# Stick-breaking attention with its row tiles taken from the last to the first

## Chip, core and metric

One core of one Trainium2 chip. The metric is the device time of one execution in microseconds (us), the median of several runs.

## What is computed

One decoder layer over 1024 prompt rows and 8 sample rows. What matters here:

```
q, k, v, u = rmsnorm(x) @ w_in            # q, k normalised per head; 8 heads of 64
z[i, j]    = q[i] . k[j] / 8 + bias       # strictly causal: j < i
a[i, j]    = sigmoid(z[i, j]) * product over j < l < i of sigmoid(-z[i, l])
h          = x + concat(a @ v, pool(u)) @ w_out
m          = rmsnorm(h)                   # then the router: top 1 of 4 groups, top 2 of 8 experts
h         += the two experts' outputs, weighted by their gates
y          = h + sigmoid(rmsnorm(h) @ w_ple_gate) * (p @ w_ple_proj)
```

## The kernel before

All rows lie in nine row tiles of 128: tile 0 holds the 8 samples, tiles 1 to 8 the prompt. The kernel has stages with a barrier of all engines between them: the projection (to 300 us), the attention stage (here), the experts (from 634 us) and a last stage (from 1245 us).

**The attention stage.** Its work is cut into units, in the list `units` (L804). A unit is (t, hp, g): the queries of row tile t (1 to 8), a pair of heads hp (0 to 3), and a group g of up to four key blocks (L808). Tiles 1 to 4 have one group and so four units each; their width is 128, 256, 384 and 512 columns. Tiles 5 to 8 have two groups and so eight units each: group 1 (width 128 to 512), then group 0 (width 512). That makes 48 units, numbered n = 0 to 47. Each unit goes through these steps:

- "scores" (L944, and the causal mask at L949 in the group that holds the diagonal) on TensorE; then four sigmoids on ScalarE (L1060, L1061); then two scans and a product on VectorE (L1134, L1139). It is done three units ahead: while unit n is finished, the scores of unit n + 3 are made.
- "turn": transposes of the weights into `p_at` on TensorE (L957), copied to `aT` by ScalarE (L1068).
- "values": the product with v into `p_o` (L967). After a tile's last unit ScalarE copies `p_o` to `mixT` ("attn", L1074).

**The jobs.** Beside the units stand nine jobs, one for each row tile: pieces 1 to 4 are the product with `w_out` in two halves of 512 columns (L993); VectorE adds the residual row (L1153) and multiplies by the norm's gain (L1155); "rows" transposes the result through `p_at` (L1006), ScalarE copies it to `hT` and takes the sum of squares (L1080, L1083), and GpSimd stores h and m to HBM (L912, L913) and loads the residual rows of the job after next (L915); piece 6 is the router's product (L1000, logits copied at L1172). Job number j is for row tile `jobs[j]`. Job j stands beside the units of one tile; in a tile of four units the pieces are spread as (1, 2), (3, 4), rows, 6; in one of eight units as 1, 2, 3, 4, nothing, rows, 6, nothing (`shares`, L823). The ninth job, j = 8, comes alone after the last unit (`tail`, L849). Every engine follows a plan written out by hand (L846 to L848): for a unit n in TensorE's order: turn n, scores n + 3, rows, pieces, values n.

**Queues.** SP's queue waits at L877 to L879 until job 7's h and m rows have landed in HBM, and only then loads `pT_raw` (L880, 1 MB), the first expert's gate and up weights (after all scores, L882) and down weights (after all values, L885), 2 MB each. When job 8's second half is multiplied (L888) it loads the second expert's three (L891 to L893). Then it stores the nine tiles of `p_times_w_ple_proj` (L900), whose products (L1016 to L1018) TensorE makes in `p_sc[T % 2]` after job 8; ScalarE copies each to `y_sb[T % 2]` (L1102), from T = 2 on only after the store of tile T - 2 has landed (L1100). VectorE meanwhile computes the routing tables (L1207 to L1268), and GpSimd gathers the first experts' rows (L927).

In job 8 ScalarE's plan holds the copy `pT_hi` (L1087), which waits for `pT_raw`, and VectorE's the difference `pT_lo` (L1158), in front of the residual add (L1153).

Of the kernel before, what the change touches and what calls it, by code (L numbers as in the profile page):

```python
# [17 lines left out]
T_ALL = 1 + SEQ // P  # L18
ROWS = T_ALL * P
AW = 512  # L20
H, HD = 8, 64
# [51 lines left out]
def build(nc, A, O):  # L73
# [20 lines left out]
    with ctx:  # L94
# [604 lines left out]
        GRP = 4  # L699
# [96 lines left out]
        at_done, at_copied, o_done, attn_copied = sem("aT_done"), sem("aT_copied"), sem("heads_done"), sem("attn_copied")  # L796
        w_done, w_copied = sem("p_w_filled"), sem("p_w_copied")
# [3 lines left out]
        s_c2 = sem("const2_loaded")  # L801


        units = [(t, hp, g) for t in range(1, T_ALL) for hp in range(H // 2) for g in reversed(range((t + GRP - 1) // GRP))]  # L804

        def unit(n):
            t, hp, g = units[n]
# [2 lines left out]

        def pair(n):
            t, hp, _ = units[n]
            return (t - 1) * (H // 2) + hp

        def last_of_pair(q):
            return max(n for n in range(len(units)) if pair(n) == q)
# [1 line left out]

        jobs = list(range(T_ALL))
        jobs_in = {t: [t - 1] for t in range(1, T_ALL)}
        shares = {4: [(1, 2), (3, 4), (5,), (6,)], 8: [(1,), (2,), (3,), (4,), (), (5,), (6,), ()]}  # L823

        def pieces_in(n):
# [12 lines left out]
        for n in range(len(units)):  # L838
            t, hp, g = units[n]
# [12 lines left out]
        fills, turns_to, n_turns = {}, {}, 0  # L852
        for what, arg in plan:
            if what == "piece":
                j, k = arg
# [13 lines left out]
        with nc.Block() as block:  # L869
# [62 lines left out]
            def _(pe):  # L932
                for what, arg in plan:
                    if what == "scores":
                        t, hp, g, blocks, w = unit(arg)
                        if arg >= 2:
                            pe.wait_ge(sig_done, arg - 1)
                        masked = blocks[-1] == t - 1
                        sc = p_sc[arg % 2]
                        half = w // 2 if w > 2 * P else w  # L940
                        for c in range(0, w, half):
                            for hh in range(2):
                                rows = slice(HD * hh, HD * hh + HD)
                                ins = pe.matmul(sc[:, hh * CHUNK + c:hh * CHUNK + c + half], qT[rows, hp, (t - 1) * P:t * P],  # L944
                                                kT[rows, hp, g * CHUNK + c:g * CHUNK + c + half], start=True,
                                                stop=not masked or c + half < w)
                        if masked:
                            for hh in range(2):
                                ins = pe.matmul(sc[:, hh * CHUNK + w - P:hh * CHUNK + w], ident_b[:], mask_b[:], start=False, stop=True)  # L949
                        ins.then_inc(sc_done, 1)  # L950
                    elif what == "turn":
                        t, hp, g, blocks, w = unit(arg)
                        pe.wait_ge(a_done, arg + 1)
                        pe.wait_ge(at_copied, turns_to["turn", arg])
                        for hh in range(2):
                            for i in range(len(blocks)):
                                ins = pe.transpose(p_at[:, hh * CHUNK + i * P:hh * CHUNK + (i + 1) * P], beta[arg % 3][:, hh, i * P:(i + 1) * P], ident[:])  # L957
                        ins.then_inc(at_done, 1)
                    elif what == "values":
                        t, hp, g, blocks, w = unit(arg)  # L960
                        if hp == 0 and t >= 2:
                            pe.wait_ge(attn_copied, t - 1)
                        pe.wait_ge(at_copied, turns_to["turn", arg] + 1)
                        for i, b in enumerate(blocks):
                            for hh in range(2):
                                h = 2 * hp + hh
                                ins = pe.matmul(p_o[HD * hh:HD * hh + HD, hp * P:(hp + 1) * P], v_sb[:, b + 1, h * HD:(h + 1) * HD],  # L967
                                                aT[arg % 2][:, hh, i, :], start=(i == 0 and blocks[-1] == t - 1),
                                                stop=(i == len(blocks) - 1 and g == 0))
                        ins.then_inc(o_done, 1)  # L970
                    elif what == "piece":
                        j, k = arg
                        T = jobs[j]

                        def begin(name):
                            if fills[j, name] > 0 and not (j == len(jobs) - 1 and name == "h1"):
                                pe.wait_ge(w_copied, fills[j, name])

                        if k in (1, 2, 3, 4):
                            n = (k - 1) // 2  # L980
                            if k == 1:
                                begin("h0")
                                pe.wait_ge(s_wout, 16 * KD)
                                if T > 0:
                                    pe.wait_ge(attn_copied, T)
                            if k == 3:
                                begin("h1")
                            for kk in range(4 * ((k - 1) % 2), 4 * ((k - 1) % 2) + 4):
                                if kk < 4:
                                    lhs = (mixT[T % 2] if T > 0 else mixT_s)[:, kk, :]  # L990
                                else:
                                    lhs = mixp[:, kk - 4, T * P:(T + 1) * P]
                                ins = pe.matmul(bank(j, f"h{n}"), lhs, w_out[:, kk, n * CHUNK:(n + 1) * CHUNK], start=(kk == 0), stop=(kk == 7))  # L993
                            if k in (2, 4):
                                ins.then_inc(w_done, 1)
                        if k == 6:
                            begin("logits")
                            pe.wait_ge(at_copied, turns_to["rows", j] + 1)
                            for kk in range(KD):
                                ins = pe.matmul(p_w[:, 0:NR], hT[:, kk, :], w_rt[:, kk, :], start=(kk == 0), stop=(kk == KD - 1))  # L1000
                            ins.then_inc(w_done, 1)
                    elif what == "rows":
                        pe.wait_ge(m_ready, 2 * arg + 2)
                        pe.wait_ge(at_copied, turns_to[what, arg])
                        for kk in range(KD):
                            ins = pe.transpose(p_at[:, kk * P:(kk + 1) * P], m_sb[arg % 2][:, kk * P:(kk + 1) * P], ident[:])  # L1006
                        ins.then_inc(at_done, 1)
# [39 lines left out]
            def _(act):  # L1047
                for what, arg in act_plan:
                    if what == "scores":
                        t, hp, g, blocks, w = unit(arg)  # L1050
# [18 lines left out]
                                       p_at[:].rearrange("p (a n) -> p a n", a=2)[:, :, 0:w], ACT.Copy).then_inc(at_copied, 1)  # L1069
                    elif what == "attn":  # L1070
                        act.wait_ge(o_done, max(n for n in range(len(units)) if units[n][0] == arg) + 1)
                        if arg >= 3:
                            act.wait_ge(w_done, fills[jobs.index(arg - 2), "h1"] + 1)
                        act.activation(mixT[arg % 2][:].rearrange("p c n -> p (c n)"), p_o[:], ACT.Copy).then_inc(attn_copied, 1)  # L1074
                    elif what == "rows":
                        j, T = arg, jobs[arg]
                        act.wait_ge(at_done, turns_to[what, arg] + 1)
                        if j >= 1:
                            act.wait_ge(w_done, fills[j - 1, "logits"] + 1)
                        act.activation(hT[:].rearrange("p c n -> p (c n)"), p_at[:], ACT.Copy).then_inc(at_copied, 1)  # L1080
                        if j >= 1:
                            act.wait_ge(h_ss, j)
                        act.activation(x_r[j % 2][:], h_sb[j % 2][:], ACT.Square, accum_out=h_sq[:, T:T + 1]).then_inc(h_ss, 1)  # L1083
                    elif what == "piece" and arg == (T_ALL - 1, 1):
                        act.wait_ge(s_pt, 16)
                        act.wait_ge(o_done, len(units))
                        act.activation(pT_hi[:], pT_raw[:], ACT.Copy).then_inc(p_hi, 1)  # L1087
                    elif what == "piece" and arg == (T_ALL - 1, 4):
                        act.wait_ge(s_wp, 16)
                        act.wait_ge(w_done, fills[T_ALL - 1, "h1"] + 1)  # L1090
                        act.activation(wp_hi[:], wp_raw[:], ACT.Copy).then_inc(p_hi, 1)

                        act.activation(h_rs[:, 1, 0:1], h_sq[:, 0:1], ACT.Sqrt)
# [984 lines left out]
```

## Time and profile before

| | us |
|---|---|
| median of 3 runs (lowest, highest) | 1370.99 (1369.13, 1376.37) |
| profiled execution, own time | 1377.2 |
| its span | 1375.4 |
| TensorE busy | 1293.3 (94%) |
| VectorE busy | 866.8 (63%) |
| ScalarE busy | 779.7 (57%) |
| GpSimd busy | 201.4 (15%) |
| mean granted TensorE clock | 0.972 of full |

The profile has a record of each instruction with its start and length, the granted clock of TensorE, and the DMAs. Full clock is 2.4 GHz; the other level it shows is half of that. A row of the timeline is: start, length, engine, line, operation, output<-inputs and shapes, the number of instructions merged, and in square brackets the idle time of the engine before it with what ended it. A 4-byte matmul shows as more than one instruction, so 16 rows of L993 are one half of a job. PEld is TensorE's weight load. SPq is SyncE's queue issuing a DMA.

### The profile page before, as it was taken

The page shows a single profiled execution, that of the slowest core. Times are in us where ns is not written, and L with a number is a line of the kernel's source. Part 1 is how long each engine was busy: PE and PEld are TensorE (multiplying, and loading weights), DVE is VectorE, ACT ScalarE, POOL GpSimd, SP SyncE. Part 2 cuts the span into 40 slices and gives each one's busy share as a digit, 9 for nine tenths or more (in the row PEclk, how much of TensorE's full clock was granted, in tenths as well). Part 3 has the DMA queues.
Part 4 walks back from the last instruction along what each step waited for, and adds up shares of the span by engine and source line. Part 5 has one row for each costly group of instructions (what it writes and reads, how often), then busy time and mean ns, then how long its engine had stood idle before and what let it go on. Part 6 is the DMA issues. An engine that isn't in the chain of part 4 may idle for free. (4 is left out here: it accounts for less than half of the span.)

```text
span 1375.4 us, 18490 instructions
## 1 busy us (share of the span) xinstructions
PE 1293.3 (94%) x6698; PEld 953.9 (69%) x6698; DVE 866.8 (63%) x787; ACT 779.7 (57%) x887; POOL 201.4 (15%) x207
## 2 busy tenths in 40 slices
PE   7999899999999999888999999999999999964998
PEld 4767576674565566556777778877777778853886
DVE  5434411123545667464888888888888888846554
ACT  5434311123445567535777777777778777834453
POOL 3001100000000000001122222222222222110000
PEclk9999899999999999999999999999999999986999
DMA  8756656461111111295799999999999999923552
GB/s 301 266 204 240 221 168 228 156 221 48 46 47 46 47 47 47 100 392 217 290 369 375 381 388 381 376 379 370 374 364 377 376 382 370 350 88 126 200 210 110
DMA packets 63866, 332.66 MB, mean 242 GB/s; under 512 B 12543, under 2 KB 12831, under 8 KB 49838
## 3 DMA queue, kind: packets, MB, share of 16 engines
q1 hardware_dynamic: 45374, 281.29, 52.7%
q0 software_dynamic: 18432, 50.56, 10.1%
q8 instruction: 38, 0.62, 0.2%
q14 instruction: 22, 0.18, 0.0%
HBM read 309.08 MB, written 39.74 MB: 254 GB/s over the span
## 5 line engine op out<-in xcount | busy, mean ns | idle before, releaser
L1336 DVE TENSOR_TENSOR w_lo<-w_gate,w_hi 128x2048 fp32r<-128x2048 f32 x64 | 146.6, 2293 | 32.8 <-ACT w_hi L1332 32.8
L1336 DVE TENSOR_TENSOR w_lo<-w_down,w_hi 128x2048 fp32r<-128x2048 f32 x64 | 146.4, 2287 | 12.4 <-ACT w_hi L1332 12.4
L1134 DVE TENSOR_TENSOR_SCAN keep<-keep 128x512 f32<-128x512 f32 (+3 forms) x96 | 88.6, 964 | 87.9 <-ACT beta L1061 87.9
L1336 DVE TENSOR_TENSOR w_lo<-w_up,w_hi 128x2048 fp32r<-128x2048 f32 x64 | 143.6, 2285 | 0.0
L407 PE MATMUL p_z<-w_in_hi,xT_hi 128*128 128x512 f32 (+1 forms) x288 | 119.7, 415 | 9.5 <-DVE w_in_lo L532 9.5
L1332 ACT ACTIVATE w_hi<-w_down 128x2048 fp32r<-128x2048 f32 x64 | 122.6, 1915 | 0.0
L1332 ACT ACTIVATE w_hi<-w_up 128x2048 fp32r<-128x2048 f32 x64 | 122.4, 1913 | 0.0
L1332 ACT ACTIVATE w_hi<-w_gate 128x2048 fp32r<-128x2048 f32 x62 | 118.5, 1913 | 0.0
L408 PE MATMUL p_z<-w_in_lo,xT_hi 128*128 128x512 f32 (+1 forms) x288 | 114.6, 398 | 0.0
L409 PE MATMUL p_z<-w_in_hi,xT_lo 128*128 128x512 f32 (+1 forms) x288 | 114.4, 397 | 0.0
L1347 PE MATMUL p_g<-w_hi,xeT_hi 128*128 128x512 f32 x256 | 104.1, 407 | 2.5 <-DVE xeT_lo L1555 2.5
L1347 PE MATMUL p_y<-w_hi,hiddenT_hi 128*128 128x512 f32 x256 | 104.1, 407 | 2.1 <-DVE hiddenT_lo L1581 2.1
L1347 PE MATMUL p_u<-w_hi,xeT_hi 128*128 128x512 f32 x256 | 102.9, 402 | 0.0
L1068 ACT ACTIVATE aT<-p_at 128x1024 f32<-128x1024 f32 (+3 forms) x48 | 39.5, 824 | 109.8 <-PE p_at L957 109.8
L1348 PE MATMUL p_g<-w_hi,xeT_lo 128*128 128x512 f32 x256 | 101.2, 395 | 0.0
L1348 PE MATMUL p_y<-w_hi,hiddenT_lo 128*128 128x512 f32 x256 | 100.9, 394 | 0.0
L1348 PE MATMUL p_u<-w_hi,xeT_lo 128*128 128x512 f32 x256 | 100.2, 392 | 0.0
L1434 POOL DMA_INDIRECT expert_rows<-y,idx_y x32 | 81.5, 2548 | 29.5 <-POOL idx_y L1431 28.2
L407 PEld LDWEIGHTS p_z<-w_in_hi,xT_hi 128*128 128x128 f32 (+1 forms) x288 | 51.8, 180 | 40.0 <-issue 27.5
L1353 PE MATMUL p_g<-w_lo,xeT_hi 128*128 128x512 f32 x256 | 70.2, 396 | 0.0
L1353 PE MATMUL p_y<-w_lo,hiddenT_hi 128*128 128x512 f32 x256 | 70.2, 397 | 0.0
L1353 PE MATMUL p_u<-w_lo,xeT_hi 128*128 128x512 f32 x256 | 68.9, 391 | 0.0
(261 smaller groups left out, 2506.1 us busy)
## 6 DMA issues: line engine op xcount, KB each, us to landing
w_gate<-in_w_experts SPq DMA_DIRECT2D x32, 2048.0 KB, 12.8
w_up<-in_w_experts SPq DMA_DIRECT2D x32, 2048.0 KB, 15.9
w_down<-in_w_experts SPq DMA_DIRECT2D x32, 2048.0 KB, 8.0
v_sb<-in_cache_kT SPq DMA_DIRECT2D x64, 256.0 KB, 6.6
w_in_raw<-in_cache_v SPq DMA_DIRECT2D x64, 256.0 KB, 3.8
xT_raw<-in_xT_all POOLq DMA_DIRECT2D x16, 512.0 KB, 5.5
y_loaded<-expert_rows SPq DMA_DIRECT2D x8, 1024.0 KB, 6.9
x_res<-in_x_all POOLq DMA_DIRECT2D x9, 512.0 KB, 5.4
```

The costliest lines, as they stand in the source:

```text
L407: pe.matmul(z, x_hi[par][:, k, r], w_hi[:, k, cs], start=(k == 0), stop=False)
L408: pe.matmul(z, x_hi[par][:, k, r], w_lo[:, k, cs], start=False, stop=False)
L409: ins = pe.matmul(z, x_lo[par][:, k, r], w_hi[:, k, cs], start=False, stop=(k == KD - 1))
L1068: act.activation(aT[arg % 2][:].rearrange("p a b n -> p a (b n)")[:, :, 0:w], p_at[:].rearrange("p (a n) -> p a n", a=2)[:, :, 0:w], ACT.C ...
L1134: ins = dve.tensor_tensor_scan(out=row, data0=row, data1=row, initial=first, op0=ALU.mult, op1=ALU.bypass)
L1332: act.activation(w_hi[slot][:], chunk_of(c, par), ACT.Copy).then_inc(hi_ready, 1)
L1336: dve.tensor_tensor(out=w_lo[slot][:], in0=chunk_of(c, par), in1=w_hi[slot][:], op=ALU.subtract).then_inc(lo_ready, 1)
L1347: pe.matmul(out, a_hi[:, k0 + k, :], w_hi[slot][:, k, :], start=(first and k == 0), stop=False)
L1348: pe.matmul(out, a_lo[:, k0 + k, :], w_hi[slot][:, k, :], start=False, stop=False)
L1353: ins = pe.matmul(out, a_hi[:, k0 + k, :], w_lo[slot][:, k, :], start=False, stop=(last and k == KC - 1))
L1434: pool.indirect_dma_start(out=y_dram, out_offset=bass.IndirectOffsetOnAxis(ap=idx_y[par][:, 0:1], axis=0), in_=y_sb[par][:], in_offset=Non ...
```

## The change

The order of the tiles is reversed: the units go from t = 8 to t = 1, and inside a tile as before. Job 0 is still the samples' tile, now beside the units of t = 8; jobs 1 to 7 are tiles 8 down to 2, each beside the units of the next lower tile; job 8, alone at the end, is tile 1. The counts in the waits follow the new numbers. No instruction is added or taken away.

```diff
-        units = [(t, hp, g) for t in range(1, T_ALL) for hp in range(H // 2) for g in reversed(range((t + GRP - 1) // GRP))]
+        units = [(t, hp, g) for t in reversed(range(1, T_ALL)) for hp in range(H // 2) for g in reversed(range((t + GRP - 1) // GRP))]
...
-            return (t - 1) * (H // 2) + hp
+            return (T_ALL - 1 - t) * (H // 2) + hp
...
-        jobs = list(range(T_ALL))
-        jobs_in = {t: [t - 1] for t in range(1, T_ALL)}
+        jobs = [0] + list(reversed(range(1, T_ALL)))
+        jobs_in = {t: [T_ALL - 1 - t] for t in range(1, T_ALL)}
...
-                        if hp == 0 and t >= 2:
-                            pe.wait_ge(attn_copied, t - 1)
+                        if hp == 0 and t < T_ALL - 1:
+                            pe.wait_ge(attn_copied, T_ALL - 1 - t)
...
-                                    pe.wait_ge(attn_copied, T)
+                                    pe.wait_ge(attn_copied, j)
...
-                        if arg >= 3:
-                            act.wait_ge(w_done, fills[jobs.index(arg - 2), "h1"] + 1)
+                        if arg + 2 < T_ALL:
+                            act.wait_ge(w_done, fills[jobs.index(arg + 2), "h1"] + 1)
```

## Rows read from the trace of the kernel before

**Rows 1.** Windows: TensorE, its loads, VectorE, ScalarE, GpSimd busy, clock, DMA share, GB/s
```profile
300.92:305.79 4.87, 4.09 (x26) 2.45 (x27) 2.94 (x10) 3.58 (x13) 1.05 (x2) 0.62 0.82 303
538.77:579.85 41.08, 37.39 (x278) 24.22 (x277) 24.64 (x24) 22.39 (x32) 1.05 (x2) 1.00 0.09 32
579.85:601.20 21.35, 17.87 (x56) 9.67 (x57) 7.89 (x9) 7.48 (x8) 1.35 (x3) 0.95 1.01 432
640.00:1200.00 560.00, 557.94 (x2569) 446.95 (x2568) 488.13 (x276) 426.75 (x337) 148.58 (x118) 1.00 0.92 367
```

**Rows 2.** Timeline of TensorE: "rows" in tiles 5, 6 and 7
```profile
446.09 1.06 PE L1006 MATMUL p_at<-ident,h_times_g 128*128 128x128 f32 x8 [1.28 <-ACT aT L1068]
...
485.09 1.06 PE L1006 MATMUL p_at<-ident,h_times_g 128*128 128x128 f32 x8 [0.81 <-ACT aT L1068]
...
526.21 1.06 PE L1006 MATMUL p_at<-ident,h_times_g 128*128 128x128 f32 x8 [0.41 <-ACT aT L1068]
```

**Rows 3.** Timeline of TensorE: the end of tile 8
```profile
569.71 1.07 PE L1006 MATMUL p_at<-ident,h_times_g 128*128 128x128 f32 x8 [1.30 <-ACT aT L1068]
...
577.97 1.09 PE L967 MATMUL p_o<-aT,v_sb 128*64 128x128 f32 x16 [1.17 <-ACT aT L1068]
...
579.85 3.67 PE L993 MATMUL p_sc<-w_out_sb,attn_mixed_T 128*128 128x512 f32 x8 [0.79 <-ACT attn_mixed_T L1074]
```

**Rows 4.** Timeline: the end of tile 1
```profile
322.86 0.44 PE L967 MATMUL p_o<-aT,v_sb 128*64 128x128 f32 x4
...
324.44 1.09 PE L1006 MATMUL p_at<-ident,h_times_g 128*128 128x128 f32 x8
...
326.74 0.41 PE L957 MATMUL p_at<-ident,beta 128*128 128x128 f32 x2 [0.84 <-ACT hT L1080]
...
327.83 2.17 PE L1000 MATMUL p_w<-w_router_sb,hT 128*128 128x36 f32 x16
...
328.75 0.53 POOL L913 DMA_DIRECT2D expert_input_rows<-h_times_g  x1
```

**Rows 5.** Timeline: job 7's last store and the load behind it
```profile
573.95 0.53 POOL L913 DMA_DIRECT2D expert_input_rows<-h_times_g  x1
...
577.75 0.33 SPq L880 DMA_DIRECT2D pT_raw<-in_p_T  x1
```

**Rows 6.** DMA issues at 594.6 to 595 and 610.5 to 616; last: us to landing
```profile
w_down<-in_w_experts SPq DMA_DIRECT2D x1, 2048.0 KB, 20.9
...
p_times_w_ple_proj<-y SPq DMA_DIRECT2D x1, 512.0 KB, 6.6
```

**Rows 7.** Timeline: the third tile's copy, and the first expert's transposes
```profile
615.91 1.02 ACT L1102 ACTIVATE y<-p_sc 128x1024 f32<-128x1024 f32 x1 [4.12 <-DMA p_times_w_ple_proj<-y]
...
634.50 1.06 PE L1449 MATMUL p_xe<-ident,x_gathered 128*128 128x128 f32 x8 [2.02 <-PEq L869]
```

**Rows 8.** Timeline: VectorE's residual adds in job 8
```profile
587.07 0.69 DVE L1153 TENSOR_TENSOR h<-p_sc,x_res 128x512 f32<-128x512 f32 x1
...
593.86 0.69 DVE L1153 TENSOR_TENSOR h<-p_sc,x_res 128x512 f32<-128x512 f32 x1 [5.38 <-PE p_sc L993]
```

**Rows 9.** Timeline: a unit of tile 8, and the first piece of job 0
```profile
545.84 0.69 ACT L1060 ACTIVATE keep<-p_sc,per_partition 128x512 f32<-128x512 f32 x1 [0.20 <-PE p_sc L949]
...
548.29 2.34 DVE L1134 TENSOR_TENSOR_SCAN keep<-keep 128x512 f32<-128x512 f32 x2 [2.10 <-ACT beta L1061]
...
550.67 1.23 DVE L1139 TENSOR_TENSOR beta<-beta,keep 128x1024 f32<-128x1024 f32 x1
...
305.79 5.19 PE L993 MATMUL p_w<-w_out_sb,attn_mixed_T_samples 128*128 128x512 f32 x8
```

**Rows 10.** Windows around three falls of the clock, columns as in rows 1
```profile
162.20:175.90 13.70, 11.92 (x31) 8.85 (x32) 0.00 (x0) 1.51 (x2) 0.00 (x0) 0.50 0.24 89
302.20:309.00 6.80, 6.02 (x20) 3.09 (x19) 4.66 (x12) 4.18 (x16) 0.17 (x1) 0.51 0.99 388
329.50:336.30 6.80, 6.80 (x21) 3.52 (x21) 5.04 (x10) 3.96 (x10) 0.31 (x1) 0.51 0.67 221
```

## The prediction

> **What bounds the kernel now.** I first read the windows by tile, cut at the first piece of each job. Tile 8's own stretch has TensorE busy 37.39 of 41.08 us, with VectorE at 24.64 and ScalarE at 22.39 [rows 1]; the other tiles look the same or fuller. So the attention stage runs at TensorE's pace, and since the change neither adds nor removes an instruction, its busy time stays. What can change is where TensorE waits, at which clock it runs, and when something that hangs on an event of the stage is released.
>
> Next I followed the stage's end to the first expert, where the time is handed on. TensorE begins the first expert's transposes at 634.50, right behind the stage's barrier [rows 7], and from 640 to 1200 us it is busy without a gap of note [rows 1], so a shift of that start goes one to one into the end. Backwards from there: ScalarE's copy of the third `p_times_w_ple_proj` tile at 615.91 waited 4.12 us for the store of the first one to land [rows 7]; the rest up to 634.50 follows from that copy and from the stores after it. That store stands on SP's queue behind the second expert's weights, of which `w_down`, issued just after 594.6, landed 20.9 us later [rows 6], near 615.6. And all that time the DMA engines were full (share 1.01 and 432 GB/s from 579.85 on [rows 1]). So the stream of `pT_raw`, six weight tensors and the first store, which begins when SP issues `pT_raw` at 577.75 [rows 5], is what sets 615.91 and through it the first expert. The tail's own chain, job 8 and the routing, ends somewhat earlier than that stream.
>
> Last I read the clock. It falls to half (1.2 GHz) for 6.8 us at 302.2 and at 329.5 [rows 10]. The first follows the thin end of the projection, the second the end of tile 1, where TensorE waits 0.84 us and makes the router's product, 16 short instructions of 36 columns [rows 4].
>
> **The change part by part.**
>
> *Waits at "rows".* TensorE's idle time before L1006 is 1.28, 0.81 and 0.41 us in tiles 5, 6 and 7 [rows 2] and 1.30 in tile 8 [rows 3]. It waits there for ScalarE's copy, and what covers the wait are the scores of unit n + 3: 256, 384 and 512 columns wide in tiles 5, 6 and 7, and none in tile 8. After the change the unit three ahead belongs to the next lower tile: 384 columns in tile 8 (0.81), 256 in tile 7 (1.28), 128 in tile 6 (some 1.5, my estimate between 1.28 and the 1.30 of no cover, and a little above for a busier ScalarE), 512 in tile 5 (0.41). The sum goes from 3.80 to 4.00. Tile 8's wait of 1.17 before its last values [rows 3] goes, as units follow it. Tile 1 is last now: between its piece 4 and its rows no scores stand any more, but rows must wait for VectorE's add and product anyway; they began 1.58 us after the piece's end (324.44 less 322.86 [rows 4]), and still will, with 0.8 us of it idle. The wait of 0.84 [rows 4] stays, and so does the 0.79 before job 8 [rows 3]. Together: 3.80 + 1.17 + 0.84 + 0.79 = 6.60 before, 4.00 + 0.80 + 0.84 + 0.79 = 6.43 after. Tiles 2 to 4 may gain or lose 0.2 us each. I take **0**, within -1.5 and +1.
>
> *The fill at the start.* Before, the first piece of `w_out` starts at 305.79, 4.87 us after the first scores, as the units are 128 wide. A unit of 512 columns takes 2.45 us from its first sigmoid to its scan (548.29 less 545.84 [rows 9]), then the scan 2.34, then the product 1.23 [rows 9]. With the scores themselves (about 1.2) ahead, turn 0 begins 7.6 us after the start, near 308.5, and piece 1, behind turn 0 and scores 3, near 311 to 313. By 309.0 TensorE before has done four small units' scores, a turn and half of piece 1, together about 3.8 us of work at full clock; afterwards three wide scores and a bit of turn 0, about 3.6. The fill falls almost wholly into the half-clock stretch [rows 10], in which before lost time too. Cost **+0.2**.
>
> *Whether the clock comes back at 309.* Before, it did, after 3.2 us of unbroken 512-column work. After the change the same time holds one wide score product and the first half us of turn 0. The nearest row is the stretch from 162.2 to 175.9, which began as thinly and stayed at half for 13.7 us, twice as long [rows 10]. If it stays here too, TensorE does 3.4 us of work in the 6.8 us up to 315.8, and as it is the bound there, **+3.4**; if not, 0. I take 3.4 as the fill is thinner than before's; both ends go into the range.
>
> *The clock at tile 1.* Before, that fall cost 3.4 us in the middle of the stage. Afterwards tile 1's end is thinner still and lies just ahead of job 8; a fall there slows job 8, which has room (next part). So against the profiled execution **-3.4**. But this credit exists only where the execution before had that fall.
>
> *When the stream starts.* This is the one large term. SP issues `pT_raw` when job 7's rows have landed. Before, job 7 stood in tile 8's wide units: 577.75 is 2.10 us ahead of job 8's first piece at 579.85. Afterwards it stands beside tile 1. From the end of piece 4, by tile 1's own rows: rows at +1.58; store of m issued at +5.9 (328.75 less 322.86 [rows 4]); landed and seen by SP 3.8 later (577.75 less 573.95 [rows 5]), so `pT_raw` at +9.7. TensorE: rows +1.58, turn at +3.9 (326.74), no scores, the router's product to +5.9, values and the `attn` copy, job 8's first piece at +7.3. The load is issued 2.4 us behind that piece instead of 2.10 ahead: **+4.5** on everything that hangs on the stream. Nothing hides it, since the DMA engines are full to its end and TensorE's own tail is earlier.
>
> *Work the late load holds up.* `pT_hi` and `pT_lo` stand ahead of the adds on ScalarE and VectorE. The first add was at 587.07, the second, which counts, at 593.86, with VectorE idle 5.38 us ahead of it [rows 8]. 4.5 us later the first add and its product still end 0.9 us before the second. Cost 0, at most 1.
>
> *Unchanged.* GpSimd's loads of residual rows still have more than a tile's time; the second weight loads are issued while the first are still landing.
>
> Sum against the profiled execution (1377.2, span 1375.4): 0 + 0.2 + 3.4 - 3.4 + 4.5 = +4.7, or 1381.9. That execution stands 6.2 us above the median, likely by falls of the clock that the median run lacked, so I don't carry its level: I put the difference on the median, 1370.99 + 4.7 = **1375.7**.
>
> **The rivals.** (A) *The clock recovers at 309* as before. Then the difference is 1.3: 1372.3. For it: the stretch at 302.2 recovered with 6.02 us busy. (B) *The slower side: the clock's account comes out with no credit.* If the usual execution before has no fall at tile 1, while the changed one keeps the half clock in the fill, it pays 0.2 + 3.4 + 4.5 = +8.1: 1379.1. It decides as soon as the credit is lost and the fill stays at half; for it speaks the gap of 6.2 us between profiled run and median. (C) *The stream isn't the bound*, because the store need not wait for the weights. Then only TensorE's own path counts: 0.2 + 3.4 - 3.4 and the shorter drain, down to -3.2 if the fill's clock recovers as well, 1367.8 to 1371.2. Against it: the store's 6.6 us and the weights' landing at the same moment [rows 6]. The Trainium skill (DMA: Bandwidth & Descriptors, "Queues, rings and completion order") says that completion isn't first in, first out per issuing engine, so a later DMA may be done before an earlier one. By that rule the case C would hold; the trace speaks for the other one here.
>
> **How the numbers follow.** Forecast case, between 3 and 6.8 us slower: 0.40. A: 0.20. B: 0.22. C: 0.13. The remaining 0.05 is for a wait I haven't seen, either way. A measurement of this kernel can tell about 0.5% from no change, that is 6.9 us. B lies mostly above that bound, C almost wholly within it. So faster 0.03, same 0.75, slower 0.22. The range holds the forecast, A, most of B and the upper part of C: 1368.5 to 1380.5.
>
> **What would show it.** In the changed profile: (1) `pT_raw` issued 2 to 3 us after job 8's first piece; (2) `p_times_w_ple_proj` copy 2 waiting longer than 4.12 us for the store, and 38.2 us after `pT_raw`'s issue as before (615.91 less 577.75); (3) job 0's first piece near 311 to 313, and half clock until 315.8; (4) no fall in the first tiles, and one at or near job 8's start; (5) VectorE's first add of job 8 near 12 us after the piece, the second unmoved. The prediction is wrong if the copy follows TensorE's product and not the store, or if idle time at "rows" adds up to more than 6 us over the tiles.

## The result, and the profile after

The changed kernel takes 1380.94 us (median of 15 runs, 1377.83 to 1383.65), the kernel before, run again beside it, 1374.45 (15 runs, 1369.13 to 1379.53). The ratio is **1.0048, with a 95% interval of 1.0038 to 1.0058**: 6.5 us slower. That is within the 0.5% that the prediction took as the smallest difference it could tell, but the interval leaves no doubt about the side. Forecast were 4.7 us more. The time lies 0.4 us above the range, since the median before was put at 1370.99 and came out 3.5 us higher. The ratios below are taken over all executions and not from the medians, so the two can differ by 0.1% (as in run 1), and two executions of the kernel before, of 5227.52 and 3264.25 us, stay out of them.

The two profiled executions differ by as much: spans of 1381.8 and 1375.4. Each took 2.7 us longer than the median of its kernel, and the changed kernel's is the slowest of its 15. The timeline of the changed kernel at the fill, which answers to [rows 9]:

```profile
299.90 1.18 PE L944 MATMUL p_sc<-kT,qT 64*128 64x256 f32 x8 [0.59 <-PEq L230]
...
307.61 1.97 PE L957 MATMUL p_at<-ident,beta 128*128 128x128 f32 x8 [1.29 <-DVE beta L1139]
309.51 1.90 PE L944 MATMUL p_sc<-kT,qT 64*128 64x256 f32 x8
...
311.34 3.70 PE L993 MATMUL p_w<-w_out_sb,attn_mixed_T_samples 128*128 128x512 f32 x8
```

The first piece comes 11.44 us after the first scores; before it was 4.87 [rows 1, 9]. The turn takes 1.97 us where a full-clock turn of this size takes 1.09: the fill runs at half clock. Windows of the changed kernel (columns as in rows 1), four stretches at half clock, to be held against [rows 10]. Two more, near 600 behind job 8 and as the first expert begins (near 642, before near 637), both kernels have:

```profile
300.90:311.10 10.20, 8.40 (x38) 5.39 (x36) 7.07 (x6) 8.17 (x13) 0.45 (x1) 0.50 0.71 281
553.40:560.20 6.80, 6.80 (x23) 3.60 (x23) 2.79 (x8) 2.74 (x9) 0.20 (x1) 0.50 0.65 215
580.80:584.20 3.40, 3.40 (x5) 1.35 (x4) 0.00 (x0) 0.00 (x0) 0.00 (x0) 0.50 0.65 192
621.70:628.50 6.80, 6.18 (x15) 4.83 (x16) 2.12 (x10) 5.84 (x5) 2.08 (x2) 0.50 0.59 187
```

The first stretch lasts 10.2 us, before 6.8. The fall at 553.4 is at the end of tile 2, the one at 580.8 in job 8. The one at 329.5 of before is gone.

The timeline at the end of tile 1 and in job 8, which answers to [rows 3, 4, 5, 8]:

```profile
573.14 0.44 PE L967 MATMUL p_o<-aT,v_sb 128*64 128x128 f32 x4
...
574.72 1.09 PE L1006 MATMUL p_at<-ident,h_times_g 128*128 128x128 f32 x8 [0.77 <-DVE h_times_g L1155]
...
577.02 0.41 PE L957 MATMUL p_at<-ident,beta 128*128 128x128 f32 x2 [0.84 <-ACT hT L1080]
...
578.99 0.53 POOL L913 DMA_DIRECT2D expert_input_rows<-h_times_g  x1
...
580.30 5.37 PE L993 MATMUL p_sc<-w_out_sb,attn_mixed_T 128*128 128x512 f32 x8 [0.79 <-ACT attn_mixed_T L1074]
582.78 0.33 SPq L880 DMA_DIRECT2D pT_raw<-in_p_T  x1
...
591.99 0.69 DVE L1153 TENSOR_TENSOR h<-p_sc,x_res 128x512 f32<-128x512 f32 x1
...
596.00 0.69 DVE L1153 TENSOR_TENSOR h<-p_sc,x_res 128x512 f32<-128x512 f32 x1 [2.60 <-PE p_sc L993]
```

`pT_raw` is issued 2.48 us behind job 8's first piece; before it was 2.10 ahead. The second add waits for TensorE still, with 2.60 us of idle time left of 5.38. And the way to the first expert, which answers to [rows 7]:

```profile
621.25 1.02 ACT L1102 ACTIVATE y<-p_sc 128x1024 f32<-128x1024 f32 x1 [7.33 <-DMA p_times_w_ple_proj<-y]
...
622.32 0.80 PE L1016 MATMUL p_sc<-w_ple_proj_hi,pT_hi 128*128 128x512 f32 x1 [2.25 <-ACT y L1102]
...
641.41 1.21 PE L1449 MATMUL p_xe<-ident,x_gathered 128*128 128x128 f32 x8 [2.02 <-PEq L869]
```

The third tile's copy waits 7.33 us for the store instead of 4.12, TensorE stands still for 2.25 us behind it, and its clock falls at 621.7. I count from the first scores of the stage, as the projection ends at a slightly different time in each execution:

| us | before | changed |
|---|---|---|
| first scores to job 8 | 278.93 | 280.40 (+1.47) |
| job 8 to issue of `pT_raw` | -2.10 | 2.48 (+4.58) |
| issue of `pT_raw` to the third copy | 38.16 | 38.47 (+0.31) |
| third copy to the first expert | 18.59 | 20.16 (+1.57) |
| first scores to the first expert | 333.58 | 341.51 (+7.93) |
| first expert to the end of the span | 740.9 | 740.4 |

The first scores came 1.02 us sooner in the changed kernel's execution, and the rest after the first expert took 0.5 less: 7.9 - 1.0 - 0.5 = 6.4, the difference of the spans.

### The profile page after: what moved, and what is told of

Its sections match the earlier page's. It is cut to its first block and busy times, and to the rows that moved or that the text cites. A ratio compares the mean times of both kernels' runs of the same rounds, so it can differ in the third digit from the quotient of the medians.

```text
span 1381.8 us, 18488 instructions
## 1 busy us (share of the span) xinstructions
PE 1297.4 (94%) x6698; PEld 955.8 (69%) x6698; DVE 866.8 (63%) x787; ACT 780.5 (56%) x887; POOL 201.3 (15%) x207
## 3 DMA queue, kind: packets, MB, share of 16 engines
q0 software_dynamic: 18432, 50.56, 10.1%
```

## The experiments

**Two theories.** S: the later start of the stream (`pT_raw`, the weights and the first store, one behind the other on SyncE's queue) is the cost. R: the cost lies on TensorE's own path, in the fill, the waits and the clock.

**Run 1: the changed kernel, gate and up weights ahead of `pT_raw`.**

```diff
+                sp.wait_ge(sc_done, len(units))
+                load_part(sp, slice(0, 1), 0, w_g[0], s_wg[0])
+                load_part(sp, slice(0, 1), 1, w_u[0], s_wu[0])
                 sp.wait_ge(s_hm[1], 32 * 4)
...
-                sp.wait_ge(sc_done, len(units))
-                load_part(sp, slice(0, 1), 0, w_g[0], s_wg[0])
-                load_part(sp, slice(0, 1), 1, w_u[0], s_wu[0])
```

> The changed kernel, but SyncE's queue issues the first expert's gate and up weights (4 MB) as soon as the last scores are made, near 556 us, and pT_raw behind them. Theory S (the stream of pT_raw, weights and first store bounds the way to the first expert, and the change starts it 4.6 us later against job 8): 4 MB or about 9.7 us of that stream are out of the way, the third tile's copy no longer waits for the store, TensorE has no 2.25 us gap and no fall of the clock there; 6 to 9 us faster than the changed kernel, 0.998 of before. Theory R (the cost is on TensorE's own path: fill, waits at rows and clock): no change against the changed kernel, 1.0048 of before.

Measured 1376.03 us, ratio to the kernel before 1.0024 (1.0008 to 1.0040): by the ratio half of the cost is gone, by the medians (1374.51 beside it) three quarters, and in either case less than S said. The third copy (ScalarE's copy of the third `p_times_w_ple_proj` tile) still waits for the store (timeline):

```profile
615.30 1.02 ACT L1102 ACTIVATE y<-p_sc 128x1024 f32<-128x1024 f32 x1 [4.96 <-DMA p_times_w_ple_proj<-y]
```

Two things hold the stream's end. `pT_raw` still goes out 2.29 us behind job 8's first piece, and the second expert's weights 16.72 us behind it, against 14.01 before, as job 8 began at half clock here (6.8 us from 575.9).

**Run 2: the kernel before with the same edit.**

> The kernel before with the same edit of SyncE's queue: gate and up weights go out when the last scores are made, near 566 us instead of 578. Theory S: the store lands earlier, the third tile's copy runs right behind its product (near 613.5 instead of 615.9), 2 to 5 us faster, 0.997 of before. Theory R: 1.000.

Measured 1373.80 us, 0.9998 (0.9986 to 1.0011): no gain, a miss for S as I had put it. SyncE's queue in its profile:

```profile
562.92 0.33 SPq L741 DMA_DIRECT2D w_gate<-in_w_experts  x1
...
579.42 0.33 SPq L883 DMA_DIRECT2D pT_raw<-in_p_T  x1
579.80 0.43 SPq L741 DMA_DIRECT2D w_down<-in_w_experts  x1
590.56 0.33 SPq L741 DMA_DIRECT2D w_gate<-in_w_experts  x1
```

The gate weights do go out 14 us ahead of job 8's first piece (576.56). But now they stand beside job 7's stores: the last was issued at 570.66 and `pT_raw` followed only 8.8 us later, where [rows 5] show 3.8. And the second expert's weights are tied to job 8's second half, at 590.56, in every order. The third copy did come 35.00 us behind job 8's first piece, against 36.06 before, but TensorE made no use of it (see run 6).

**Run 3: the kernel before, the stream held back.**

```diff
                 sp.dma_start(pT_raw[:] ...).then_inc(s_pt, 16)
+                sp.wait_ge(w_done, fills[T_ALL - 1, "h0"] + 1)
                 sp.wait_ge(sc_done, len(units))
```

> The kernel before, the first expert's weights held back until job 8's first half is multiplied, 8.8 us later than before; pT_raw goes out as before. Theory S: the stream ends up to 8.8 us later and all behind it with it: 7 to 10 us slower, 1.006. Theory R: these weights are read only 30 us later, so nothing: 1.000.

Measured 1383.12 us, 1.0059 (1.0042 to 1.0076), some 8 us: a pure delay of the weights by 8.8 us, with the order of the tiles untouched, costs nearly its own length. R falls as a sole cause. In its profile the third copy comes 7.0 us later behind job 8 than before and TensorE's next product 6.1 us; the other 2.2 of the 8.35 us to the first expert come behind that, where TensorE ran at half clock. Its profile shows the pattern of the changed kernel, only larger (timeline, then a window at half clock):

```profile
622.88 1.02 ACT L1103 ACTIVATE y<-p_sc 128x1024 f32<-128x1024 f32 x1 [11.12 <-DMA p_times_w_ple_proj<-y]
...
623.96 0.80 PE L1017 MATMUL p_sc<-w_ple_proj_hi,pT_hi 128*128 128x512 f32 x1 [5.97 <-ACT y L1103]
...
642.82 1.46 PE L1450 MATMUL p_xe<-ident,x_gathered 128*128 128x128 f32 x8 [2.02 <-PEq L869]
```
```profile
619.40:629.60 10.20, 5.64 (x13) 4.47 (x14) 2.30 (x11) 5.76 (x5) 2.08 (x2) 0.50 0.72 227
```

**Run 4: tiles 7, 6, 5, 4, 3, 2, 1, 8.** The order is a list here, and the waits count by its positions.

```diff
+        order = [7, 6, 5, 4, 3, 2, 1, 8]
+        units = [(t, hp, g) for t in order for hp in range(H // 2) for g in reversed(range((t + GRP - 1) // GRP))]
...
+        jobs = [0] + order
+        jobs_in = {t: [order.index(t)] for t in order}
```

> Tiles in the order 7, 6, 5, 4, 3, 2, 1, 8: the fill is wide as in the changed kernel, the end is tile 8 as in the kernel before. Theory S: pT_raw is again issued 2 us ahead of job 8's first piece, only the fill costs, 0 to 3.4 us: 1.000 to 1.0025. Theory R, if the fill and its clock are the cost: 1.0048.

Measured 1375.15 us, 1.0000 (0.9989 to 1.0012). `pT_raw` went out 2.06 us ahead of job 8, and a fill of 384 and 512 columns cost nothing that shows, though the clock stayed at half for 10.2 us there: job 8 began 278.98 us after the first scores, before 278.93.

**Run 5: tiles 2, 8, 7, 6, 5, 4, 3, 1.**

> Tiles in the order 2, 8, 7, 6, 5, 4, 3, 1: the fill is narrow (256 columns), the end is tile 1 as in the changed kernel. Theory S: pT_raw is issued some 2.5 us behind job 8's first piece, the third tile's copy waits for the store, 4.5 to 6.5 us slower than before: 1.004. Theory R, if the fill and its clock are the cost: 1.000.

Measured 1378.00 us, 1.0024 (1.0012 to 1.0036), half of the changed kernel's loss. Its profile, of the slowest of 12 executions, suggests why it is less than 4.5 us: the stream is late by the same amount (`pT_raw` 2.49 us behind job 8, third copy with 7.37 us of waiting, the first expert 59.18 us behind job 8 against 54.65), but job 8 itself starts 1.34 us sooner after the first scores (277.59). 4.53 less 1.34 is 3.2 us, or 0.23%.

**Runs 6 and 7: the second expert's weights behind the seventh store**, in the kernel before and in the changed kernel.

```diff
                 sp.wait_ge(at_done, turns_to["turn", len(units) - 1] + 1)
-                load_part(sp, slice(1, 2), 0, w_g[1], s_wg[1])
-                load_part(sp, slice(1, 2), 1, w_u[1], s_wu[1])
-                load_part(sp, slice(1, 2), 2, w_d[1], s_wd[1])
...
                     sp.dma_start(pp_dram[T * P:(T + 1) * P, :][r, :], y_sb[T % 2][r, :]).then_inc(s_pp[T % 2], 16)
+                    if T == 6:
+                        load_part(sp, slice(1, 2), 0, w_g[1], s_wg[1])
+                        load_part(sp, slice(1, 2), 1, w_u[1], s_wu[1])
+                        load_part(sp, slice(1, 2), 2, w_d[1], s_wd[1])
```

> The kernel before, with the second expert's three weight tensors (6 MB) issued behind the seventh store of p_times_w_ple_proj instead of ahead of the first. Theory S: the stream is over 15 us before the first store, so the third tile's copy follows its product (near 613.5), and the first expert starts 3 to 6 us earlier: 0.997. If the second expert's weights come too late the gain is lost in a gap before expert 1. Theory R: 1.000.

> The changed kernel with the same edit. Theory S: the later start of the stream has 15 us of room now, so nothing of the 4.6 us is left; the copy doesn't wait, the clock doesn't fall there, and the kernel lies within 0 to 3 us of the previous run (fill and clock on TensorE's own path), 0.998 of before. Theory R: all of the change's 6.5 us stay over the previous run: 1.002.

Run 6: 1374.36 us, 1.0000 (0.9990 to 1.0009). Run 7: 1377.04 us, **1.0019 (1.0003 to 1.0034)**, below the changed kernel's 1.0048 with no overlap of the intervals. Giving the late stream room takes away 0.29%, 4.0 us, of the change's cost, and does nothing for the kernel before. The 12 executions of run 7 fall into two groups: five at 1372.28 to 1374.12 us with a mean granted clock of 0.973 to 0.975, and seven at 1376.46 to 1381.76 with 0.967 to 0.971. The profile is one of the first group (1372.96). Job 8 begins 278.78 us after the first scores in it and the first expert 333.60 after them, as before (278.93 and 333.58), though the fill was at half clock for twice as long as before:

```profile
297.20:310.90 13.70, 11.84 (x46) 7.29 (x47) 8.89 (x11) 9.17 (x15) 1.05 (x2) 0.51 0.56 209
```

So in this execution nothing of the cost is left. The later start of the stream (`pT_raw` 2.49 us behind job 8's first piece) is there and costs nothing, and the long fill costs no more than the short one and the fall at tile 1 did together.

Run 6's profile says why the kernel before gains nothing (timeline):

```profile
610.62 1.03 ACT L1103 ACTIVATE y<-p_sc 128x1024 f32<-128x1024 f32 x1 [1.89 <-PE p_sc L1019]
...
614.46 0.61 PE L1042 MATMUL p_at<-block_onehots,rank_onehots 128*128 128x32 bf16 x18 [0.58 <-DVE rank_onehots L1245]
...
620.77 1.03 ACT L1103 ACTIVATE y<-p_sc 128x1024 f32<-128x1024 f32 x1 [1.77 <-PE p_sc L1019]
623.57 1.03 ACT L1103 ACTIVATE y<-p_sc 128x1024 f32<-128x1024 f32 x1 [1.77 <-PE p_sc L1019]
```

The third copy no longer waits for a store; it runs 33.83 us behind job 8, against 36.06. But TensorE must wait for VectorE's one-hots before the product of the slot table, 37.67 us behind job 8 here, and then makes five more products of 2.8 us each; the first expert is 54.38 behind job 8, against 54.65. A second chain, through VectorE's routing, ends at nearly the same time as the stream. The kernel before shows it too: at 617.38 TensorE had waited for the one-hots, and the next product began at 617.85, 0.92 us after the third copy (615.91 and 1.02 long, [rows 7]) had ended:

```profile
617.38 0.62 PE L1041 MATMUL p_at<-block_onehots,rank_onehots 128*128 128x32 bf16 x18 [0.58 <-DVE rank_onehots L1244]
...
617.85 0.47 PE L1016 MATMUL p_sc<-w_ple_proj_hi,pT_hi 128*128 128x512 f32 x1
```

Making the stream earlier gains nothing, making it later costs what goes beyond these 0.92 us. The profiles side by side, in us behind job 8's first piece:

| | third copy ends | next product on TensorE | first expert |
|---|---|---|---|
| run 6 | 34.86 | 38.13 | 54.38 |
| run 7 | 35.28 | 38.58 | 54.82 |
| before | 37.08 | 38.00 | 54.65 |
| changed | 41.97 | 42.02 | 61.11 |
| run 5 | 42.01 | 42.07 | 59.18 |
| run 3 | 44.08 | 44.14 | 63.00 |

In the upper three the product follows the one-hots, in the lower three the copy.

**Run 8: tiles 8, 6, 5, 4, 3, 2, 1, 7**, for the 0.19% that stay in run 7's ratio.

> Tiles in the order 8, 6, 5, 4, 3, 2, 1, 7: the same fill of 512 columns as in the changed kernel, but a wide end with pT_raw issued ahead of job 8. Open is the part of 0.19% that stays when the stream has room. If it is the fill and the clock behind it: 1.0015 to 1.0025. If it is the narrow end: 1.000.

Measured 1377.23 us, 1.0015 (1.0003 to 1.0028). By the ratio alone this would point to the fill, but it doesn't separate the two: this order also issued `pT_raw` only 0.76 us ahead of job 8, 1.3 later than before. In its profile job 8 begins 0.93 us later after the first scores than before, and the first expert another 1.12 us later behind job 8, so over half of the loss lies behind the fill.

**Run 9: run 5's order with the late second weights**, the candidate to beat both.

> Tiles in the order 2, 8, 7, 6, 5, 4, 3, 1 (the fill narrow, the end tile 1), with the second expert's weights behind the seventh store. Without the late weights this order lay at 1.0024 and reached job 8 1.3 us earlier than the kernel before. If the late stream was all of its cost: 0.999, faster than both kernels by a little. If the narrow end and the clock there cost by themselves: 1.001 to 1.002.

Measured 1374.83 us, 1.0003 (0.9989 to 1.0016): level with the kernel before, and 0.21% under run 5. That fits the late stream as the whole cost of this order, though the two intervals just overlap. It isn't faster: job 8 starts at 277.44 after the first scores, 1.5 sooner than before, but runs its first 3.4 us at half clock, and the first expert follows 56.29 us behind it instead of 54.65: the routing chain starts from job 8's result and is late with it (TensorE's next product at 40.02 us behind job 8, before 38.00). No version here beats the kernel before.

## Why the prediction was right or wrong

The side and the main term were right. What put the time outside the range was the base of the sum, the median of three executions (1370.99), with 1374.45 from fifteen; from that base the same +4.7 gives 1379.2, still 1.8 us short. The steps of the sum that failed are the credit of 3.4 us for the clock at tile 1, which the changed kernel's profile does not show, and the shift behind the third copy, put at the delay alone, where the profile shows 1.57 us more. Against them stands the +3.4 for the fill, which was too large.

- **The base: wrong.** The profiled execution stood 6.2 us above 1370.99, and I put that down to falls of the clock that the median execution lacked. Against fifteen executions it stands 2.75 us above, and the fall at tile 1 is in all four profiles of the old order (before, runs 2, 3 and 6).
- **When the stream starts: right.** 4.5 us forecast, 4.58 in the profile, by the steps named: rows at +1.58 (574.72 less 573.14), store of m at +5.85, `pT_raw` 3.79 later. Run 3 shows that such a delay counts, and run 7 that giving it room takes away 4.0 of the 6.5 us. The third copy came 4.89 us later behind job 8, and 4.02 of that reached TensorE's next product (42.02 against 38.00).
- **What bounds the kernel before: wrong.** I wrote that the stream is what sets the first expert and that the tail's own chain ends somewhat earlier. Its own profile shows the reverse order at the third copy, by 0.92 us (the rows beside run 6), and run 6 shows that the two chains give the same first expert within 0.3 us. For a later stream the sum is off only by that 0.92; for an earlier one the statement fails, as in runs 2 and 6.
- **What follows the late copy: the term that was missing.** I let everything after the third copy shift by the delay alone. It took 1.57 us more (20.16 against 18.59), and the copy itself 0.31. TensorE stands still for 2.25 us and then makes products in a stretch of 6.8 us at half clock. In two profiles the clock falls in such a wait (the changed kernel's and run 3's, 19.94 us from copy to expert); in run 5's profile ScalarE's wait was the same and TensorE stood still for 1.89 us, but there was no fall, and its copy-to-expert time was 18.19. So it is seen and not shown: no run tests the wait as the cause of the fall, nor the fall by itself.
- **The clock at tile 1: the credit was wrong.** I took 3.4 us off because the fall at tile 1 would move into job 8, where it is covered. In the profile a fall came at the end of tile 2 (553.4), ahead of the stream's start, where it isn't covered, and another in job 8. With the +3.4 for the fill I had +0.2 for the whole way to job 8; measured +1.47. The fill did stay at half clock, for 10.2 us, but that ended as the first wide piece began, so that only scores and one turn were slowed. By the windows TensorE lost 1.8 us idle and half of 8.40 busy there, 6.0 in all, before 0.8 and half of 6.02, 3.8 in all: some 2.2 more, my estimate, where 3.6 were forecast. The fall at the end of tile 2 is not in every execution: run 7's profile, with the same order of tiles, lacks it, and job 8 begins 278.78 us after the first scores. Nor is job 8 always cover for a fall. Here the late stream covered it; in run 9, where the stream had room, the first expert came 1.64 us later behind job 8.
- **When the fill ends: right.** Turn 0 was forecast 7.6 us after the first scores (the terms named beside it add up to 7.2) and came at 7.71; the first piece was forecast between 10.1 and 12.1 behind them and came at 11.44.
- **Waits at "rows":** forecast 0.81, 1.28, 1.5 and 0.41 in tiles 8, 7, 6 and 5. Measured 0.23, 0.84, 1.27 and 0.85, together 3.19 against my 4.00 and 3.80 before. The rule (the cover is the scores of the unit three ahead) holds for the order of tiles 8 to 6, not for tile 5; the term stays small.
- **Work behind `pT_raw`: right.** The second add still waited for TensorE. It came 15.70 us behind job 8's first piece, before 14.01, as the piece ran at half clock.
- **The rivals.** A (the clock recovers at once) did not come true in the profile. B (no credit) was forecast at +8.1 and its number lies nearest to the 6.5, but not for its reason: it asked for a kernel before without the fall at tile 1, and the four profiles of the old order all have it. The credit was lost by a new fall at tile 2, and the fill was cheaper than its 3.4. C (the stream doesn't bind, as the store need not wait for the weights) is refuted by runs 3 and 7; in the kernel before the stream does stand back, by 0.92 us, but behind the routing chain and not for C's reason. The Trainium skill's rule behind C (DMA: Bandwidth & Descriptors, "Queues, rings and completion order"), that a later DMA may complete before an earlier one, isn't contradicted by these runs, but it gave the first store no way past the weights here: the third copy's wait for it grew with their delay, from 4.12 to 7.33 and 11.12 us.
- **The range** failed by 0.4 us because it hung on the median of three runs, 1370.99; fifteen gave 1374.45. Its upper end was 9.5 us above the base; set on 1374.45 it would have been 1383.95.

What stays open: where the last 0.19% (2.6 us) lie. They are in the slower seven of run 7's executions, whose mean granted clock is lower, and no profile of one of them was taken. Falls at the narrow tile ends, as at the end of tile 2, would fit; that is argued, not shown.

## What to carry to other kernels

Reversing a loop changes no busy time, but it changes what the last iteration is, and everything that the next stage triggers from "the last but one job is stored" moves with it: find the loads gated so, and measure their issue against the path that runs beside them. Before counting on a gain from an earlier transfer, look for a second chain that ends at the same point; two chains in balance punish a delay and don't reward a lead. The profile of the kernel before can show it: look at what TensorE waited for last, and at how long the freed buffer had stood ready when it was used. And a median of three runs is too thin a base for a range of some us.

## What was unexpected

A wait of 2 us on TensorE between products may cost more than itself: in the changed kernel the clock fell at the end of 2.25 us of standing still and stayed at 0.50 for 6.8 us, in run 3 it fell during 5.97 us and stayed there for 10.2; in run 5, after 1.89 us, it did not fall. And moving 4 MB of loads ahead of small stores went with slower stores in run 2: the store that SyncE waits for landed 8.8 us after its issue instead of 3.8.
